# Moving the split weight pieces inside their ring rows, and x and the masks with them, in a four-layer decoder trunk

## The chip, the cores and the metric

The kernel runs on one core of one Trainium2 chip. The metric is the device time of one execution in microseconds (us). Engines are named as the profile names them: PE is TensorE (matmuls), PEld its weight loads, DVE is VectorE, ACT is ScalarE, POOL is GpSimd, SP is SyncE, which here issues most DMA transfers. L560 is line 560 of the kernel before.

## The reference, cut to what matters

The trunk has four layers on a (1, 256, 1024) float32 input. Each layer is an FFN, a token mixer and another FFN; every one of these twelve sub-layers is wrapped in two RMSNorms:

```
x = x + 0.5 * rmsnorm(swiglu(rmsnorm(x, g0), wg, wu, wd), g1)      # FFN, D_FF = 2816
x = x + rmsnorm(mixer(rmsnorm(x, g2)), g3)                         # conv, attention, mLSTM, conv
x = x + 0.5 * rmsnorm(swiglu(rmsnorm(x, g4), wg, wu, wd), g5)
```

The conv mixer projects to 3 x 1024, gates, convolves with three taps and projects out. The attention mixer projects to three groups of q, k and v (16 heads of 64), attends in three dilated causal windows, mixes them by their log-sum-exp and projects out. The mLSTM mixer projects to q, k, v, an output gate and eight gate columns, runs a stabilised matrix memory and projects out. All weights are float32.

## The kernel before

**Split products.** Every float32 weight and activation is split into a high part (rounded to the type fp32r) and a low part (the rest). One product is three fp32r matmuls: high by high, high by low, low by high. A matmul has a stationary operand (loaded 128x128, PEld) and a moving operand (256 or 512 columns), and the weight load of the next matmul runs while the present one streams its moving operand.

**Pieces and rings.** All weights come as one stream of 352 pieces of 128 x 2048 float32 (`PIECE` = 2048 words a partition). SP loads piece p into `raw[p % 3]`. ACT writes its high part to `w_high[p % 6]` (L1215), DVE writes `raw - w_high` to `w_low[p % 6]` (L1660), PE multiplies, and the semaphores `piece_high`, `piece_split` and `piece_used` keep the order. `RING` is 6, and before the change a ring row is exactly one piece, 8192 bytes a partition.

**Two ways round.** A piece is multiplied in one of two ways. *Features-first*: the weights are stationary and x (`xT_both`, which holds the transposed high and low x, 256 tokens) is the moving operand; so run the blocks of the FFNs (`block`, L560 to L562) and most pieces of the mixers (`features_half`, L574 to L576). *Tokens-first*: 128 tokens of x are stationary and the piece's columns move. In the mixers these are 256 columns (`tokens_first`, L574 to L576, and `arriving`, L587 to L593); in the FFNs the first four pieces (`early_block`, L560 to L562 and `arriving`) with 512 columns. Tokens-first pieces are: the first three of each mixer (`first_three`), the v pieces of attention (three of nine in each quarter, the first three of quarter 0 among them) and pieces 7 to 11 of mLSTM. The down and output projections move weights of 512 columns past `oT_hi` and `oT_lo`; they are not touched.

**Where things lie.** SBUF tensors are allocated in order: `raw`, `w_high`, `w_low`, `oT_hi`, `oT_lo`, `x`, `xn`, `gain`, each a multiple of 8192 bytes a partition, then six small ones that take 32 bytes each, then `xT_both`. So `xT_both` begins 192 bytes (48 words) past a multiple of 8192 from the start of each ring row, and `oT_hi` at a multiple. In mLSTM alone, `X_SHIFT` puts x 32 words (128 bytes) further into `xT_both`.

**The turn of x.** At a sub-layer's start the second 128 tokens of x are still being normed. PE runs two and a half tokens-first pieces on the first tile, waits for `xn` (L1708 on DVE, the end of a chain over ACT, DVE and POOL), makes eight transposes (L609), and goes on. `products_at_entry` (L568 to L570) is a form of the product that cuts the first of its three matmuls into two of 128 columns; it is used at a few places behind transposes or a change of piece, in `first_three` for mLSTM alone.

**Masks and gains.** `att_mask`, `ml_mask` and `tri` are loaded by SP behind the twelfth piece. ACT loads two gain vectors in each joint (`load_gains`, L1337 and L1339).

Of the kernel before, what the change touches and what calls it, by code (L numbers as in the profile page):

```python
# [24 lines left out]
F32R = mybir.dt.float32r  # L25
# [3 lines left out]
P = 128  # L29
# [46 lines left out]
X_SHIFT = {"ffn": 0, "conv": 0, "att": 0, "ml": 32}  # L76
# [68 lines left out]

def build(nc, x_in, gains, first_gain, stream, gate_w, gate_b, conv_k, ident_in, rope_in, att_mask_in, ml_mask_in,
          tri_in, out):
    with ExitStack() as ctx:
# [10 lines left out]
        w_high = sb("w_high", [P, RING, PIECE], F32R)  # L159
        w_low = sb("w_low", [P, RING, PIECE], F32R)  # L160
# [65 lines left out]
        ml_mask = sb("ml_mask", [P, 2 * P])  # L226
        tri = sb("tri", [P, P])
# [23 lines left out]
        loaded = sem("loaded")  # L251
        raw_landed = [sem(f"raw_landed{n}") for n in range(RAW)]
# [87 lines left out]
        CONSTS = 16 * 7  # L340
# [177 lines left out]
        def _(sp):  # L518
# [13 lines left out]
            sp.dma_start(ml_mask[:, :], ml_mask_in).then_inc(loaded, 16)  # L532
            sp.dma_start(tri[:, :], tri_in).then_inc(loaded, 16)
# [19 lines left out]
        def _(pe):  # L553
# [24 lines left out]
            def arriving(acc, joint, t, half, p, width, first_col):  # L578


                tok, slot = slice(t * P, (t + 1) * P), p % RING
# [4 lines left out]
                for k, cols in rows:  # L586
                    nc.tensor.matmul(acc, xT_high()[:, k, tok], w_high[:, slot, cols], start=k == 0, stop=False)  # L587
                x_ready(joint, t, half)
                for k, cols in rows:
                    nc.tensor.matmul(acc, xT_low()[:, k, tok], w_high[:, slot, cols], start=False, stop=False)  # L590
                weights_ready(p)
                for k, cols in rows:
                    last = nc.tensor.matmul(acc, xT_high()[:, k, tok], w_low[:, slot, cols], start=False, stop=k == KD - 1)  # L593
# [27 lines left out]
            def ffn(sub):  # L621
# [13 lines left out]
                def early_block(i, first_x=False, meanwhile=None):  # L635
# [3 lines left out]
                    for half in range(2):  # L639
                        p = w0 + early_piece(c) + half  # L640
                        slot = p % RING
# [4 lines left out]
                        for k in () if first_x else range(4 * half, 4 * half + 4):  # L646
# [3 lines left out]
                                            w_high[:, slot, cols], w_low[:, slot, cols], k == 0, k == KD - 1)  # L650
# [7 lines left out]
                def block(i, p, turn=0):  # L658
# [3 lines left out]
                    for e in range(2):  # L662
                        for k in range(KD):
                            cols = slice(k * 256 + e * P, k * 256 + (e + 1) * P)
                            last = products(ps[:, gu_bank(i), e * SEQ:(e + 1) * SEQ], w_high[:, p % RING, cols],
                                            w_low[:, p % RING, cols], xT_high()[:, k, :], xT_low()[:, k, :],
                                            k == 0, k == KD - 1)
                    last.then_inc(piece_used, 1)

                def first_blocks():  # L670

                    x0, slot = slice(0, P), 0
# [3 lines left out]
                    for k, cols in rows[0:2]:  # L676
                        nc.tensor.matmul(ps[:, GU_BANK, :], xT_high()[:, k, x0], w_high[:, slot, cols], start=k == 0, stop=False)
                    transpose_x(0, 1)
                    x_ready(0, 0, 0)
                    for k, cols in rows[0:2]:  # L680
                        nc.tensor.matmul(ps[:, GU_BANK, :], xT_low()[:, k, x0], w_high[:, slot, cols], start=False, stop=False)
                    pe.wait_ge(piece_high, 1)
                    for k, cols in rows[2:4]:
                        nc.tensor.matmul(ps[:, GU_BANK, :], xT_high()[:, k, x0], w_high[:, slot, cols], start=False, stop=False)
                        nc.tensor.matmul(ps[:, GU_BANK, :], xT_low()[:, k, x0], w_high[:, slot, cols], start=False, stop=False)
                    pe.wait_ge(first_split, 1)
                    for k, cols in rows:
                        if k == 2:
                            weights_ready(0)
                        nc.tensor.matmul(ps[:, GU_BANK, :], xT_high()[:, k, x0], w_low[:, slot, cols], start=False, stop=False)  # L690
# [14 lines left out]
                def seven(c, some, turn=0):  # L705
# [11 lines left out]
                    for n in some:  # L717
# [7 lines left out]
                        else:  # L725
                            rh, rl = w_high[:, p % RING, cols], w_low[:, p % RING, cols]
# [1642 lines left out]
```

## Time and profile before

| what | value |
|---|---|
| median of 3 runs | 1981.74 us (1981.50 to 1982.76) |
| the profiled execution | 1981.68 us, span 1979.1 us |
| PE busy | 1971.2 us |
| DVE busy | 1619.8 us |
| ACT busy | 1103.9 us |

The profiled execution took 1981.68 us as timed; its span, from the first to the last instruction, is 1979.1 us, so 2.58 us lie around the span. [...] A line of the source view gives a line's instructions in a stretch: count, smallest, median and largest duration in ns, and the start of the first and of the last. In mixers three matmuls lie between two starts of L574 (the three parts of a product).

### The profile page before, as it was taken

The page shows a single profiled execution, that of the slowest core. Times are in us where ns is not written, and L with a number is a line of the kernel's source. Part 1 is how long each engine was busy: PE and PEld are TensorE (multiplying, and loading weights), DVE is VectorE, ACT ScalarE, POOL GpSimd, SP SyncE. Part 2 cuts the span into 40 slices and gives each one's busy share as a digit, 9 for nine tenths or more (in the row PEclk, how much of TensorE's full clock was granted, in tenths as well). Part 3 has the DMA queues.
Part 4 walks back from the last instruction along what each step waited for, and adds up shares of the span by engine and source line. Part 5 has one row for each costly group of instructions (what it writes and reads, how often), then busy time and mean ns, then how long its engine had stood idle before and what let it go on. Part 6 is the DMA issues. An engine that isn't in the chain of part 4 may idle for free.

```text
span 1979.1 us, 36338 instructions
## 1 busy us (share of the span) xinstructions
PE 1971.2 (100%) x14806; PEld 1839.8 (93%) x14806; DVE 1619.8 (82%) x1865; ACT 1103.9 (56%) x1208; POOL 26.5 (1%) x52
## 2 busy tenths in 40 slices
PE   9999999999999999999999999999999999999998
PEld 8999989998999999988998999998999899998998
DVE  8988678888888777769898888657888888777886
ACT  6555445555555665666555556645555555545553
POOL 0000000000000000000000000000000000000000
PEclk9999999999999999999999999999999999999999
DMA  7655645564555644435555556534556456654552
GB/s 265 246 212 202 228 170 192 193 243 159 210 212 196 213 172 153 168 129 191 213 200 208 189 196 248 215 130 149 213 192 233 171 207 227 215 183 157 213 191 107
DMA packets 56289, 386.35 MB, mean 195 GB/s; under 512 B 6752, under 2 KB 7136, under 8 KB 11232
## 3 DMA queue, kind: packets, MB, share of 16 engines
q1 hardware_dynamic: 52416, 372.07, 51.6%
q10 hardware_dynamic: 3744, 12.39, 2.0%
q8 instruction: 102, 1.67, 0.3%
q14 instruction: 27, 0.22, 0.0%
HBM read 383.39 MB, written 1.05 MB: 194 GB/s over the span
## 4 chain that ended last, share of the span: by engine, by line
PE 97%; DVE 1%; DMA 1%; issue 0%; ACT 0%; POOL 0%; DVEq 0%; POOLq 0%; SPq 0%
PE ps L560 21%; PE ps L561 21%; PE ps L562 21%; PE ps L574 6%; PE ps L575 6%; PE ps L576 6%; PE ps L590 2%; PE ps L587 2%; PE ps L593 2%; PE ps L739 1%; PE ps L736 1%; PE ps L735 1%; PE ps L609 1%; PE ps L965 0%; PE ps L700 0%
## 5 line engine op out<-in xcount | busy, mean ns | idle before, releaser
L1660 DVE TENSOR_TENSOR w_low<-raw,w_high 128x2048 fp32r<-128x2048 f32 x272 | 616.3, 2286 | 87.4 <-ACT w_high L1215 87.4
L560 PE MATMUL ps<-xT_both,w_high 128*128 128x256 f32 x2304 | 638.4, 277 | 0.0
L561 PE MATMUL ps<-xT_both,w_high 128*128 128x256 f32 x2304 | 637.1, 277 | 0.0
L562 PE MATMUL ps<-xT_both,w_low 128*128 128x256 f32 x2304 | 636.6, 276 | 0.0
L1215 ACT ACTIVATE w_high<-raw 128x2048 fp32r<-128x2048 f32 x279 | 530.6, 1912 | 39.9 <-DMA raw<-stream 27.4
L561 PEld LDWEIGHTS ps<-xT_both,w_high 128*128 128x128 f32 x2304 | 433.3, 188 | 0.0
L562 PEld LDWEIGHTS ps<-xT_both,w_low 128*128 128x128 f32 x2304 | 432.7, 188 | 0.0
L560 PEld LDWEIGHTS ps<-xT_both,w_high 128*128 128x128 f32 x2304 | 432.5, 188 | 0.1
L1261 ACT ACTIVATE region<-ps 128x256 f32<-128x256 f32 x176 | 67.4, 383 | 439.2 <-PE ps L562 431.7
L574 PE MATMUL ps<-xT_both,w_high 128*128 128x256 f32 x729 | 204.9, 281 | 0.0
L575 PE MATMUL ps<-xT_both,w_low 128*128 128x256 f32 x729 | 202.6, 278 | 0.0
L576 PE MATMUL ps<-xT_both,w_high 128*128 128x256 f32 x729 | 202.5, 278 | 0.0
L1733 DVE TENSOR_TENSOR region<-region,ps 128x256 f32<-128x256 f32 x176 | 73.8, 419 | 131.9 <-ACT region L1261 129.6
L560 PE MATMUL ps<-w_high,oT_hi 128*128 128x512 f32 x456 | 179.1, 393 | 0.0
L561 PE MATMUL ps<-w_low,oT_hi 128*128 128x512 f32 x456 | 177.9, 390 | 0.0
L562 PE MATMUL ps<-w_high,oT_lo 128*128 128x512 f32 x456 | 177.9, 390 | 0.0
L1292 ACT ACTIVATE w_high<-xn 128x2048 fp32r<-128x2048 f32 x72 | 138.2, 1919 | 27.3 <-DVE xn L1773 25.8
L1786 DVE TENSOR_TENSOR w_low<-xn,w_high 128x2048 fp32r<-128x2048 f32 x64 | 146.4, 2287 | 4.8 <-ACT w_high L1292 4.8
L574 PEld LDWEIGHTS ps<-xT_both,w_high 128*128 128x128 f32 x729 | 137.3, 188 | 0.7
L575 PEld LDWEIGHTS ps<-xT_both,w_low 128*128 128x128 f32 x729 | 137.2, 188 | 0.0
L576 PEld LDWEIGHTS ps<-xT_both,w_high 128*128 128x128 f32 x729 | 137.0, 188 | 0.0
L1779 DVE TENSOR_TENSOR corner<-raw,corner 128x1536 fp32r<-128x1536 f32 x72 | 126.1, 1752 | 0.0
(239 smaller groups left out, 3140.3 us busy)
## 6 DMA issues: line engine op xcount, KB each, us to landing
raw<-stream SPq DMA_DIRECT2D x351, 1024.0 KB, 4.8
gain<-gains ACTq DMA_DIRECT2D x23, 512.0 KB, 4.9
x<-x_in SPq DMA_DIRECT2D x2, 512.0 KB, 4.5
raw<-stream SPq DMA_DIRECT2D x2, 512.0 KB, 6.2
region<-rope_in SPq DMA_DIRECT2D x1, 512.0 KB, 5.1
out<-x SPq DMA_DIRECT2D x1, 512.0 KB, 2.6
att_mask<-att_mask_in SPq DMA_DIRECT2D x1, 320.0 KB, 5.5
out<-x SPq DMA_DIRECT2D x1, 256.0 KB, 2.1
```

The lines of the kernel that those rows point to most:

```text
L560: nc.tensor.matmul(acc, lh, rh, start=start, stop=False, skip_group_check=goes_on)
L561: nc.tensor.matmul(acc, lh, rl, start=False, stop=False, skip_group_check=goes_on)
L562: return nc.tensor.matmul(acc, ll, rh, start=False, stop=stop, skip_group_check=goes_on)
L574: nc.tensor.matmul(acc, lh, rh, start=start, stop=False)
L575: nc.tensor.matmul(acc, ll, rh, start=False, stop=False)
L576: return nc.tensor.matmul(acc, lh, rl, start=False, stop=stop)
L1215: nc.scalar.activation(w_high[:, p % RING, :], raw[:, p % RAW, :], ACT.Copy).then_inc(piece_high, 1)
L1292: nc.scalar.activation(w_high[:, p % RING, :], sums, ACT.Copy).then_inc(piece_high, 1)
L1660: nc.vector.tensor_tensor(w_low[:, p % RING, :], raw[:, p % RAW, :], w_high[:, p % RING, :], ALU.subtract).then_inc(piece_split, 1)
L1733: nc.vector.tensor_tensor(h_of(i) if i >= EARLY else h[:, i % 2, :], silu[:, i % 2, :], ps[:, gu_bank(i), SEQ:2 * SEQ], ALU.mult).then_inc ...
L1779: nc.vector.tensor_tensor(corner[:, c % 2, 1, :], raw[:, p % RAW, HALF:4 * HALF], corner[:, c % 2, 0, :], ALU.subtract).then_inc(piece_spl ...
L1786: nc.vector.tensor_tensor(w_low[:, p % RING, :], sums, w_high[:, p % RING, :], ALU.subtract).then_inc(sums_split, 1)
```

## The change

- A ring row gets 64 words (256 bytes) more: `ROW = PIECE + 64`, for `w_high` and `w_low`. A piece begins in its row at `w_shift(p)`: 41 words (164 bytes) in for the first four pieces of an FFN, 32 words (128 bytes) for tokens-first pieces of mixers, 0 for all others. ACT, DVE and PE use that place through `high_of(p)` and `low_of(p)`.
- x lies at the start of `xT_both` in every sub-layer; mLSTM's 32 words are gone (the tensor keeps its size).
- `products_at_entry` is used at the turn of x in conv and attention too (`halves_at=4 if turns`), and at the start of mLSTM's feature pieces 4, 5 and 6 (`i > 3`).
- `ml_mask` and `tri` have no tensors of their own: they are views of `att_mask`, loaded by ACT in the joint behind attention, after the last masking (`masked`), ahead of the gains there. SP has two constant loads fewer, and DVE and PE wait for `masks_landed` in mLSTM.

```diff
-X_SHIFT = {"ffn": 0, "conv": 0, "att": 0, "ml": 32}
+X_PAD = 32
+ROW = PIECE + 64
+W_SHIFT = {"early": 41, "tokens": 32}
...
+def w_shift(p):
+
+    sub = max(n for n in range(SUBLAYERS) if BASE[n] <= p)
+    q, kind = p - BASE[sub], KINDS[sub]
+    if kind == "ffn":
+        return W_SHIFT["early"] if q < EARLY else 0
+    if kind == "att":
+        tokens = q < QP * QUARTERS and not 1 <= ATT_ORDER[q // QP][q % QP] <= QK
+    else:
+        tokens = q < 3 or kind == "ml" and 7 <= q < 12
+    return W_SHIFT["tokens"] if tokens else 0
...
-        w_high = sb("w_high", [P, RING, PIECE], F32R)
-        w_low = sb("w_low", [P, RING, PIECE], F32R)
+        w_high = sb("w_high", [P, RING, ROW], F32R)
+        w_low = sb("w_low", [P, RING, ROW], F32R)
+
+        def place(p):
+
+            first = w_shift(p)
+            return slice(first, first + PIECE)
+
+        def high_of(p):
+            return w_high[:, p % RING, place(p)]
+
+        def low_of(p):
+            return w_low[:, p % RING, place(p)]
...
-        xT_both = sb("xT_both", [P, 2 * KD * SEQ + max(X_SHIFT.values())], F32R)
+        xT_both = sb("xT_both", [P, 2 * KD * SEQ + X_PAD], F32R)
...
-            at = X_SHIFT[KINDS[sub_now[0]]] + which * KD * SEQ
-            return xT_both[:, at:at + KD * SEQ].rearrange("p (k c) -> p k c", k=KD)
+            return xT_both[:, which * KD * SEQ:(which + 1) * KD * SEQ].rearrange("p (k c) -> p k c", k=KD)
...
-        ml_mask = sb("ml_mask", [P, 2 * P])
-        tri = sb("tri", [P, P])
+        ml_mask = att_mask[:, 0:2 * P]
+        tri = att_mask[:, 2 * P:3 * P]
...
-            sp.dma_start(ml_mask[:, :], ml_mask_in).then_inc(loaded, 16)
-            sp.dma_start(tri[:, :], tri_in).then_inc(loaded, 16)
...
-                        done = tokens_first(p % RING, acc, t, meanwhile=(lambda: transpose_x(sub, 1)) if turns else None,
-                                            halves_at=4 if turns and KINDS[sub] == "ml" else None)
+                        done = tokens_first(p, acc, t, meanwhile=(lambda: transpose_x(sub, 1)) if turns else None,
+                                            halves_at=4 if turns else None)
...
-                    features_first((w0 + i) % RING, bank).then_inc(piece_used, 1)
+                    features_first(w0 + i, bank, i > 3).then_inc(piece_used, 1)
...
                 pe.wait_ge(ml_copied, 6)
+                pe.wait_ge(masks_landed, 32)
...
-                nc.scalar.activation(w_high[:, p % RING, :], raw[:, p % RAW, :], ACT.Copy).then_inc(piece_high, 1)
+                nc.scalar.activation(high_of(p)[:, :], raw[:, p % RAW, :], ACT.Copy).then_inc(piece_high, 1)
...
+                if joint and KINDS[joint - 1] == "att":
+                    act.wait_ge(masked, 4 * QUARTERS)
+                    act.dma_start(ml_mask, ml_mask_in).then_inc(masks_landed, 16)
+                    act.dma_start(tri, tri_in).then_inc(masks_landed, 16)
                 act.dma_start(gain[:, 0, :], gains[2 * joint + 1].partition_broadcast(P)).then_inc(gain_landed, 16)
...
                 dve.wait_ge(loaded, CONSTS)
+                dve.wait_ge(masks_landed, 32)
```

Every other line of the diff puts `high_of(p)` or `low_of(p)` where `w_high[:, p % RING, ...]` or `w_low[:, p % RING, ...]` stood.

## Rows read from the trace of the kernel before

**Rows 1.** The page: busy time in us of each engine, share of the span, instructions.
```profile
PE 1971.2 (100%) x14806; PEld 1839.8 (93%) x14806; DVE 1619.8 (82%) x1865; ACT 1103.9 (56%) x1208; POOL 26.5 (1%) x52
```

**Rows 2.** The page, chain that ended last: shares of the span by engine.
```profile
PE 97%; DVE 1%; DMA 1%; issue 0%; ACT 0%; POOL 0%; DVEq 0%; POOLq 0%; SPq 0%
```

**Rows 3.** Waits of PE: for whom, us in total, times, longest us.
```profile
PE ps L609 <- DVE xn L1708: 0.2, 1, 0.2
```

**Rows 4.** Source view of L574, first conv: a tokens-first, then a features-first stretch.
```profile
L574 PE MATMUL ps<-w_high,xT_both x16: 279/279/279, 199.8 to 205.1; 128*128 128x256 f32 x16
...
L574 PE MATMUL ps<-xT_both,w_high x92: 276/276/276, 212.0 to 243.0; 128*128 128x256 f32 x92
```

**Rows 5.** Source view of L574, mLSTM: tokens-first, two features-first stretches, tokens-first.
```profile
L574 PE MATMUL ps<-w_high,xT_both x16: 276/276/276, 1258.5 to 1263.6; 128*128 128x256 f32 x16
...
L574 PE MATMUL ps<-xT_both,w_high x16: 276/276/276, 1265.8 to 1270.9; 128*128 128x256 f32 x16
...
L574 PE MATMUL ps<-xT_both,w_high x15: 278/280/280, 1272.0 to 1277.0; 128*128 128x256 f32 x15
...
L574 PE MATMUL ps<-w_high,xT_both x15: 281/281/281, 1303.3 to 1308.2; 128*128 128x256 f32 x15
```

**Rows 6.** Source view of L574: conv behind transposes, attention's features, attention's tokens-first.
```profile
L574 PE MATMUL ps<-xT_both,w_high x31: 281/281/281, 245.0 to 255.6; 128*128 128x256 f32 x31
...
L574 PE MATMUL ps<-xT_both,w_high x74: 276/276/276, 657.9 to 682.7; 128*128 128x256 f32 x74
...
L574 PE MATMUL ps<-w_high,xT_both x16: 279/279/387, 741.7 to 747.1; 128*128 128x256 f32 x16
```

**Rows 7.** Timeline of PE (start us, us): early blocks, then down projection, of sub-layer 2.
```profile
297.14 0.39 PE L560 MATMUL ps<-w_high,xT_both 128*128 128x512 f32 x1
...
301.72 0.39 PE L562 MATMUL ps<-w_high,xT_both 128*128 128x512 f32 x1
...
443.16 0.39 PE L560 MATMUL ps<-w_high,oT_hi 128*128 128x512 f32 x1
...
447.70 0.39 PE L562 MATMUL ps<-w_high,oT_lo 128*128 128x512 f32 x1
```

**Rows 8.** Timelines of DVE and PE at the turn of x: conv, mLSTM, an FFN.
```profile
193.24 1.29 DVE L1708 SCALAR_TENSOR_TENSOR xn<-x,rstd_x,gain 128x1024 f32<-128x1024 f32 x1 [0.66 <-POOL rstd_x L2256]
...
194.62 1.05 PE L609 MATMUL ps<-ident,xn 128*128 128x128 f32 x8
...
1252.03 1.28 DVE L1708 SCALAR_TENSOR_TENSOR xn<-x,rstd_x,gain 128x1024 f32<-128x1024 f32 x1 [0.66 <-POOL rstd_x L2256]
...
1253.38 1.09 PE L609 MATMUL ps<-ident,xn 128*128 128x128 f32 x8
...
284.64 1.28 DVE L1708 SCALAR_TENSOR_TENSOR xn<-x,rstd_x,gain 128x1024 f32<-128x1024 f32 x1 [0.66 <-POOL rstd_x L2256]
...
287.54 1.03 PE L609 MATMUL ps<-ident,xn 128*128 128x128 f32 x8
```

**Rows 9.** Timeline of PE behind those transposes: conv without the cut, mLSTM with it.
```profile
195.44 0.36 PE L574 MATMUL ps<-w_high,xT_both 128*128 128x256 f32 x1
...
195.87 0.28 PE L574 MATMUL ps<-w_high,xT_both 128*128 128x256 f32 x1
...
1254.22 0.42 PE L568 MATMUL ps<-w_high,xT_both 128*128 128x128 f32 x2
...
1254.77 0.28 PE L574 MATMUL ps<-w_high,xT_both 128*128 128x256 f32 x1
```

**Rows 10.** Timelines of ACT and PE in the joint behind attention.
```profile
902.46 0.97 ACTq L1339 DMA_DIRECT2D gain<-gains  x1
...
904.16 0.39 ACT L1261 ACTIVATE region<-ps 128x256 f32<-128x256 f32 x1 [1.42 <-PE ps L562]
...
909.67 0.38 PE L700 MATMUL ps<-ident,region 128*128 128x128 f32 x2
```

**Rows 11.** Source view of the conv's shifted taps on DVE, L2025.
```profile
L2025 DVE SCALAR_TENSOR_TENSOR region<-region,conv_kT x32: 476/481/485, 218.0 to 1772.9; 128x256 f32<-128x256 f32 x32
```

More of the change, by code:

```diff
@@ L338, in build @@
         stored = sem("stored")
-        CONSTS = 16 * 7
+        CONSTS = 16 * 5
         used[0] = 0
@@ L586, in arriving @@
                 for k, cols in rows:
-                    nc.tensor.matmul(acc, xT_high()[:, k, tok], w_high[:, slot, cols], start=k == 0, stop=False)
+                    nc.tensor.matmul(acc, xT_high()[:, k, tok], high_of(p)[:, cols], start=k == 0, stop=False)
                 x_ready(joint, t, half)
                 for k, cols in rows:
-                    nc.tensor.matmul(acc, xT_low()[:, k, tok], w_high[:, slot, cols], start=False, stop=False)
+                    nc.tensor.matmul(acc, xT_low()[:, k, tok], high_of(p)[:, cols], start=False, stop=False)
                 weights_ready(p)
                 for k, cols in rows:
-                    last = nc.tensor.matmul(acc, xT_high()[:, k, tok], w_low[:, slot, cols], start=False, stop=k == KD - 1)
+                    last = nc.tensor.matmul(acc, xT_high()[:, k, tok], low_of(p)[:, cols], start=False, stop=k == KD - 1)
                 return last
@@ L664, in block @@
                             cols = slice(k * 256 + e * P, k * 256 + (e + 1) * P)
-                            last = products(ps[:, gu_bank(i), e * SEQ:(e + 1) * SEQ], w_high[:, p % RING, cols],
-                                            w_low[:, p % RING, cols], xT_high()[:, k, :], xT_low()[:, k, :],
+                            last = products(ps[:, gu_bank(i), e * SEQ:(e + 1) * SEQ], high_of(p)[:, cols],
+                                            low_of(p)[:, cols], xT_high()[:, k, :], xT_low()[:, k, :],
                                             k == 0, k == KD - 1)
@@ L670, in first_blocks @@
                 def first_blocks():
-                    x0, slot = slice(0, P), 0
+                    x0, p = slice(0, P), 0
                     rows = [(k, slice(k * 512, (k + 1) * 512)) for k in range(4)]
@@ L676, in first_blocks @@
                     for k, cols in rows[0:2]:
-                        nc.tensor.matmul(ps[:, GU_BANK, :], xT_high()[:, k, x0], w_high[:, slot, cols], start=k == 0, stop=False)
+                        nc.tensor.matmul(ps[:, GU_BANK, :], xT_high()[:, k, x0], high_of(p)[:, cols], start=k == 0, stop=False)
                     transpose_x(0, 1)
@@ L680, in first_blocks @@
                     for k, cols in rows[0:2]:
[L681 removed]
+                        nc.tensor.matmul(ps[:, GU_BANK, :], xT_low()[:, k, x0], high_of(p)[:, cols], start=False, stop=False)
                     pe.wait_ge(piece_high, 1)
                     for k, cols in rows[2:4]:
[L684 to L685 removed]
+                        nc.tensor.matmul(ps[:, GU_BANK, :], xT_high()[:, k, x0], high_of(p)[:, cols], start=False, stop=False)
+                        nc.tensor.matmul(ps[:, GU_BANK, :], xT_low()[:, k, x0], high_of(p)[:, cols], start=False, stop=False)
                     pe.wait_ge(first_split, 1)
@@ L689, in first_blocks @@
                             weights_ready(0)
-                        nc.tensor.matmul(ps[:, GU_BANK, :], xT_high()[:, k, x0], w_low[:, slot, cols], start=False, stop=False)
+                        nc.tensor.matmul(ps[:, GU_BANK, :], xT_high()[:, k, x0], low_of(p)[:, cols], start=False, stop=False)
                     arriving(ps[:, GU_BANK + 1, :], 0, 1, 0, 0, 512, 0).then_inc(piece_used, 1)
@@ L793, in chunk @@
                             transpose_next(sub, (1,))
-                            return nc.tensor.matmul(acc, oT_lo[:, at, tok], w_high[:, p % RING, cols], start=False, stop=True,
+                            return nc.tensor.matmul(acc, oT_lo[:, at, tok], high_of(p)[:, cols], start=False, stop=True,
                                                     skip_group_check=True)
                         last = products(ps[:, Y_BANK + 2 * t + half, :], oT_hi[:, at, tok], oT_lo[:, at, tok],
-                                        w_high[:, p % RING, cols], w_low[:, p % RING, cols], False, ends, goes_on=True)
+                                        high_of(p)[:, cols], low_of(p)[:, cols], False, ends, goes_on=True)
                     return last
@@ L820, in project_out @@
                     for q in range(first if t == 0 else 0, OUT_PIECES):
-                        slot = (p0 + q) % RING
-                        weights_ready(p0 + q)
+                        p = p0 + q
+                        weights_ready(p)
                         if t == 0 and q % 2 == 0:
@@ L835, in project_out, with features_half @@
                             last.then_inc(y_ready, 1)
-            def features_half(slot, acc, j, behind_transposes=False):
+            def features_half(p, acc, j, behind_transposes=False):
                 for k in range(KD):
@@ L856, in tokens_first @@
                     multiply = products_at_entry if k == halves_at else products_in_turn
-                    last = multiply(acc, xT_high()[:, k, tok], xT_low()[:, k, tok], w_high[:, slot, cols],
-                                    w_low[:, slot, cols], k == 0, k == KD - 1)
+                    last = multiply(acc, xT_high()[:, k, tok], xT_low()[:, k, tok], high_of(p)[:, cols],
+                                    low_of(p)[:, cols], k == 0, k == KD - 1)
                     if meanwhile and k == 3:
```

54 lines of the change are left out of this document (27 added, 27 removed).

## The prediction, made before the change was run

> **What bounds the kernel now.** The page comes first: PE is busy for 1971.2 of 1979.1 us [rows 1], and the chain that ended last lies on PE for 97% [rows 2]. The waits of PE say whether another engine holds it up: behind its start it waits once, 0.2 us, for `xn` at the turn of x in mLSTM [rows 3]. So a matmul that starts 1 ns sooner is worth up to 1 ns, except where a wait stands ready to take it. PE's durations overlap and tell little, so the third view is the source view of single lines, for the distance between starts. There the same 256-column matmul runs at two paces:
>
> - First conv, tokens-first: 5.3 us over 15 x 3 matmuls, 117.8 ns each; features-first: 31.0 over 273, 113.6 ns [rows 4]. The recorded duration marks the pace too: 279 to 281 ns in the slow one, 276 in the fast.
> - mLSTM, where x lies 32 words further, has it the other way round: tokens-first 5.1/45 = 113.3 ns; features-first fast at first (113.3), then slow (5.0/42 = 119) [rows 5].
>
> The reader should see one quantity behind both: how far, modulo 64 words, the moving operand lies from the stationary operand that is being loaded for the next matmul. x begins 48 words past a ring row (modulo 64), so features-first (x moves) has 48 and tokens-first (weights move) has -48 = 16. With x 32 words further it is 80 = 16 for features-first and -80 = 48 for tokens-first. So 48 tends to the fast pace and 16 to the slow. It is a tendency: a stretch keeps the pace it came in with. Features at 16 stayed fast for a whole piece behind a fast one [rows 5]; features at 48 ran slow at 10.6/90 = 117.8 ns behind transposes and at 24.8/219 = 113.2 ns behind a cut product; attention's tokens-first matmuls at 16 are slow behind its scores (the 387 ns is the first one) [rows 6], and one of mLSTM's token stretches at 48 is slow too [rows 5].
>
> **The change part by part.** After it, x at 0 and weights at 32 give tokens-first 16 + 32 = 48 in all mixers, features-first 48 everywhere, and the FFNs' early pieces 16 + 41 = 57. I take the difference of the paces as 4.5 ns (117.8 - 113.3).
>
> *FFN early pieces.* 96 matmuls of 512 columns in each of 8 FFNs. At 16 they take (301.72 - 297.14)/20 = 229.0 ns; the down projection, the same shape at distance 0, (447.70 - 443.16)/20 = 227.0 [rows 7]. No row has 57. It lies between 48 and 64, which is 0 again, 7 words from the 0 that is fast, so I take 227: 768 x 2.0 ns = 1.5 us. Bounds: nothing, and about 2 us if the few slow ones behind each interruption go too. The cover: the transposes there start 1.6 us behind the end of L1708 (284.64 + 1.28, then 287.54) [rows 8], so no wait takes it back.
>
> *First three pieces of conv (twice) and attention, before the turn.* Some 58 matmuls could give 0.26 us, but the norm chain does not get shorter. In conv L1708 ends at 194.53 and the transposes start at 194.62, 0.09 us behind; in mLSTM, which already runs fast here, they start 0.07 us behind and PE has waited [rows 8]. So 0.02 us is to be had, three times: 0.06 us. The stall of mLSTM appears in the others.
>
> *The same pieces behind the turn.* 81 matmuls at 4.5 ns: 0.36 us. The cut product comes in: from its start to the next product 0.55 us in mLSTM against 0.43 uncut in conv [rows 9], so it costs 0.12. Net 0.24, three times: 0.7 us. Bounds 0 and 1.1.
>
> *Attention's later v pieces.* Nine pieces, 432 matmuls. Read the same way, six stretches with 240 matmuls are slow now, of which one row stands here [rows 6]; the others came in fast and stay so. 240 x 4.5 ns = 1.1 us if all turn. They come behind scores, and at 48 a stretch can still come in slow [rows 5, 6]; I take half, 0.5 us, and 0 and 1.1 as bounds.
>
> *mLSTM.* Three of four feature pieces, 138 matmuls, are slow at 16 [rows 5]; at 48 with a cut at their start they may turn: 0.6 us, against 3 x 0.12 = 0.36 us for the cuts. A cut has been followed by a fast stretch where no transposes stood before it and by a slow one behind eight transposes [rows 6]; piece 4 has two small ones before it, piece 5 six small f32 products, piece 6 eight. I take two of three: 0.42 - 0.36 = 0.06, and 0.15 for the token piece behind them. Together 0.2 us, bounds -0.36 and 0.7.
>
> *At nothing.* The DVE and ACT writes at odd words: the conv taps read `cu` 0, 1 and 2 words in and take 476 to 485 ns all the same [rows 11]; if a row of weights were slower by some ns, DVE (82% busy) hides it. Masks: two more issues on ACT in the joint behind attention, up to 0.97 us each as the second gain took there, so 1.94 us. ACT is free from 903.43 (902.46 + 0.97) to 904.16, where PE releases the silu [rows 10]; the silu comes up to 1.2 us late. What is made of it is next needed by the transposes at 909.67 [rows 10], 5.1 us behind the end of the silu, so PE does not see it; without that cover the 1.2 us would count. `masked` was reached before the joint, and the masks land hundreds of us ahead of mLSTM, so their two waits are free. SP has two issues fewer, early, where PE does not wait.
>
> Sum: 1.5 + 0.06 + 0.7 + 0.5 + 0.2 = 3.0 us. From the profiled execution's 1981.68 us that is 1978.7; the median, 1981.74, differs by 0.06, so I predict 1978.7 us, 0.15% faster. A measurement of this kernel can tell about 0.2% (4.0 us) from no change, so this counts as the same.
>
> **The rivals.** *More of the slow pace goes.* All 240 and all 138 turn, the token stretches of mLSTM with them (95 x 4.5 = 0.4), and FFN takes 2: 2.0 + 0.8 + 1.1 + 0.6 + 0.4 - 0.36 = 4.5 us, 1977.2. And since a stretch hands its pace on, attention's features that are slow now could follow (some 440 at 4.5 ns, 2 us): 1975.2. For it speaks that fast stretches last for 219 matmuls and more [rows 6], against it that most of attention's stretches begin behind an interruption, which 48 does not cure.
>
> *Place does not matter.* The paces would come from what ran before and not from where things lie. Then only the six cuts are left, 0.7 us: 1982.4. Rows 4 and 5 speak against it, since the swap of the two ways in mLSTM would be an accident; the hysteresis in rows 5 and 6 speaks for it. [...]
>
> *Rows of odd slots go slow.* I took the relation as repeating every 64 words; rows before show only distances whose step of 128 is harmless. With 256 bytes more a row, features-first in every second slot gets 48 - 64 = -16. If the relation repeats only after 128 words, that is a distance that no row shows. It concerns half of the features-first matmuls (48 a piece: 144 pieces in the FFNs' blocks, 18 in the convs, 24 in attention, 4 in mLSTM, 9120 in all): 4560 x 4.5 ns = 20.5 us, less the gain, 1999.2. It decides the sign once some 670 of them (3.0 us / 4.5 ns) are slow. Against it: under 128 words, 0 and 48 are fast and only 80 slow, and -16 lies beside 0.
>
> **How the numbers follow.** The forecast, 1.5 to 4 us saved: 0.44. More of the slow pace goes: 0.37, nearly all past 4 us. Place does not matter, or its gain is under 1.5 us: 0.11. Odd slots slow: 0.08. So faster by over 0.2%: 0.37; within 0.2%: 0.54; slower: 0.09, the last hundredth for a wait I overlook. The range, 1975.0 to 1982.4, takes in the three cases on the fast side and their bounds and leaves out the odd slots. The forecast's own range is 1977.7 to 1980.2.
>
> **What would show it.** Right: the source view has 276 ns and 113 to 114 ns pace for tokens-first in both convs; the early pieces run at 227; PE waits 0.2 us for L1708 in conv and attention too; L568, two records a cut, has six more at the turns of x and six more in mLSTM. Wrong: L574 stays at 279 behind the turn (the cut did not help); the early pieces stay at 229 (57 is not like 0); FFN blocks at 281 in every second slot (the third rival); L700 at about 909.67 late against its block (the masks' issues).

## The result and the profile after

The changed kernel takes 1986.12 us (median; 1985.73 to 1987.01) against 1981.74 for the kernel before, which ran on the same chips: ratio 1.0022, 95% interval 1.0015 to 1.0030. It is slower by 4.4 us, where 3 us less were forecast, and outside the range.

The page of the changed kernel, busy time and chain, beside [rows 1, 2]:

```profile
PE 1976.9 (100%) x14812; PEld 1841.4 (93%) x14812; DVE 1620.2 (82%) x1865; ACT 1104.6 (56%) x1208; POOL 26.6 (1%) x52
...
PE 99%; issue 0%; DVE 0%; DMA 0%; ACT 0%; POOL 0%; DVEq 0%; POOLq 0%
```

The span grew by 5.3 us (1984.4 against 1979.1) and PE's busy time by 5.7, with six matmul records more, the six cuts. The busy times of the others grew by 1.6 us or less. PE's waits (for whom, us in total, times, longest us):

```profile
PE ps L580 <- DVE ones L1681: 1.1, 1, 1.1
PE ps L633 <- DVE xn L1733: 0.3, 1, 0.3
PE ps L700 <- ACT xT_both L1266: 0.3, 1, 0.3
```

They come to 1.7 us, all in the kernel's first 11 us, where the same view of before lists 2.5. So nobody holds PE up more than before; the matmuls themselves start further apart. In the changed kernel lines 560 to 562 are 584 to 586, 574 to 576 are 598 to 600, 587 to 593 are 611 to 617, and 609 is 633. The timeline of PE over the early pieces of sub-layer 2 (start us, recorded us): the first of them, two that stand for those of [rows 7], and the first features-first matmul behind them.

```profile
279.43 1.11 PE L611 MATMUL ps<-w_high,xT_both 128*128 128x512 f32 x4
...
298.52 0.40 PE L584 MATMUL ps<-w_high,xT_both 128*128 128x512 f32 x1
...
303.25 0.40 PE L586 MATMUL ps<-w_high,xT_both 128*128 128x512 f32 x1
...
303.62 0.37 PE L584 MATMUL ps<-xT_both,w_high 128*128 128x256 f32 x1
```

Between 298.52 and 303.25 lie 20 distances of 236.5 ns (the records of 0.40 us overlap), where [rows 7] had 229.0. From the first early matmul to the first features-first one it is 303.62 - 279.43 = 24.19 us. Call this length S; it holds the 96 early matmuls and the few transposes between them, the same in every kernel. Its two ends before the change:

```profile
278.62 1.07 PE L587 MATMUL ps<-w_high,xT_both 128*128 128x512 f32 x4
...
302.09 0.37 PE L560 MATMUL ps<-xT_both,w_high 128*128 128x256 f32 x1
```

Before the change S is 302.09 - 278.62 = 23.47 us, and 23.44 to 23.49 in the six other FFNs behind the first. After it, it is 0.69 to 0.73 us longer in each of the seven, 5.0 us in all, or 0.72 us / 96 = 7.5 ns a matmul. In the first FFN, whose S varies with the kernel's start (below), it is 0.75 us longer. With it the sum is 5.75 us, the span's whole growth and 0.4 us more.

The mixers' turn and their stretches: the first conv's timeline of DVE and PE at the turn (beside [rows 8, 9]), then the source views of L598 in the first conv (tokens, features behind them), attention (two tokens-first stretches) and mLSTM (tokens ahead of the turn and behind it).

```profile
194.09 1.28 DVE L1736 SCALAR_TENSOR_TENSOR xn<-x,rstd_x,gain 128x1024 f32<-128x1024 f32 x1 [0.66 <-POOL rstd_x L2285]
...
195.43 1.09 PE L633 MATMUL ps<-ident,xn 128*128 128x128 f32 x8
196.28 0.42 PE L592 MATMUL ps<-w_high,xT_both 128*128 128x128 f32 x2
...
196.82 0.28 PE L598 MATMUL ps<-w_high,xT_both 128*128 128x256 f32 x1
```
```profile
L598 PE MATMUL ps<-w_high,xT_both x18: 276/276/276, 197.2 to 205.7; 128*128 128x256 f32 x18
...
L598 PE MATMUL ps<-xT_both,w_high x17: 276/281/286, 206.7 to 212.8; 128*128 128x256 f32 x17
...
L598 PE MATMUL ps<-w_high,xT_both x16: 281/281/283, 685.7 to 691.0; 128*128 128x256 f32 x16
...
L598 PE MATMUL ps<-w_high,xT_both x15: 276/276/277, 734.0 to 738.7; 128*128 128x256 f32 x15
...
L598 PE MATMUL ps<-w_high,xT_both x12: 281/281/281, 1252.7 to 1256.6; 128*128 128x256 f32 x12
...
L598 PE MATMUL ps<-w_high,xT_both x18: 276/276/276, 1258.6 to 1267.1; 128*128 128x256 f32 x18
```

Tokens-first in the first conv runs fast now, as forecast (276 for the 279 of [rows 4]), but the features behind it came in slow. In attention one stretch turned from slow to fast and others from fast to slow; mLSTM's first tokens became slow. Paces changed places.

The FFNs' features-first blocks, source view of L584 in the last FFN, all slots of the ring:

```profile
L584 PE MATMUL ps<-xT_both,w_high x128: 276/276/286, 1836.6 to 1899.1; 128*128 128x256 f32 x128
```

And the engines' granted clock, in a window of those blocks in sub-layer 2 (stretch; its length; busy us and count of PE, PEld, DVE, ACT, POOL; granted clock; DMA share; GB/s):

```profile
310.00:330.00 20.00, 20.00 (x140) 18.48 (x139) 19.22 (x19) 12.94 (x10) 0.00 (x0) 1.00 0.50 180
```

It is 1.00, as in the same window of before (1.00), so the loss isn't one of the clock.

### The profile page after: what moved, and what is told of

It reads as the page before. It is cut to its first block, busy times and chain, and to the rows that moved or that the text cites. A ratio compares the mean times of both kernels' runs of the same rounds, so it can differ in the third digit from the quotient of the medians.

```text
span 1984.4 us, 36350 instructions
## 1 busy us (share of the span) xinstructions
PE 1976.9 (100%) x14812; PEld 1841.4 (93%) x14812; DVE 1620.2 (82%) x1865; ACT 1104.6 (56%) x1208; POOL 26.6 (1%) x52
## 4 chain that ended last, share of the span: by engine, by line
PE 99%; issue 0%; DVE 0%; DMA 0%; ACT 0%; POOL 0%; DVEq 0%; POOLq 0%
PE ps L584 22%; PE ps L586 22%; PE ps L585 22%; PE ps L598 6%; PE ps L600 6%; PE ps L599 6%; PE ps L614 2%; PE ps L611 2%; PE ps L617 2%; PE ps L762 2%; PE ps L758 1%; PE ps L759 1%; PE ps L633 1%; PE ps L988 0%; PE ps L723 0%
## 5 line engine op out<-in xcount | busy, mean ns | idle before, releaser
L1688 DVE TENSOR_TENSOR w_low<-raw,w_high 128x2048 fp32r<-128x2048 f32 x272 | 616.3, 2286 | 89.8 <-ACT w_high L1239 89.8
L584 PE MATMUL ps<-xT_both,w_high 128*128 128x256 f32 x2304 | 638.1, 277 | 0.0
L1239 ACT ACTIVATE w_high<-raw 128x2048 fp32r<-128x2048 f32 x279 | 530.7, 1912 | 42.1 <-DMA raw<-stream 29.4
L584 PEld LDWEIGHTS ps<-xT_both,w_high 128*128 128x128 f32 x2304 | 432.5, 188 | 0.0
L598 PE MATMUL ps<-xT_both,w_high 128*128 128x256 f32 x726 | 203.7, 281 | 0.0
L584 PE MATMUL ps<-w_high,oT_hi 128*128 128x512 f32 x456 | 179.1, 393 | 0.0
L598 PEld LDWEIGHTS ps<-xT_both,w_high 128*128 128x128 f32 x726 | 136.6, 188 | 0.7
```

Of the source, the lines that this page charges most:

```text
L584: nc.tensor.matmul(acc, lh, rh, start=start, stop=False, skip_group_check=goes_on)
L598: nc.tensor.matmul(acc, lh, rh, start=start, stop=False)
L1239: nc.scalar.activation(high_of(p)[:, :], raw[:, p % RAW, :], ACT.Copy).then_inc(piece_high, 1)
L1688: nc.vector.tensor_tensor(low_of(p)[:, :], raw[:, p % RAW, :], high_of(p)[:, :], ALU.subtract).then_inc(piece_split, 1)
```

## The experiments

The theories of each run stand in its expectation. Times are medians with the ratio to the kernel before on the same chip; where only one time is given, it is a single one and the lengths S carry the verdict. Beside these runs the kernel before took 1981.35 to 1981.64 us. Gains and losses of an FFN are its S less the S of the same FFN before. The first FFN's S is left out of verdicts, since the kernel's start lies in it: in the four kernels below with its early pieces at 0 it came out between 0.36 us shorter and 0.33 us longer than before.

**Early pieces back at 0** (rest of the change kept), and **rows and masks alone** (mixers, x and cuts as before too).

```diff
-W_SHIFT = {"early": 41, "tokens": 32}
+W_SHIFT = {"early": 0, "tokens": 32}
```
```diff
-W_SHIFT = {"early": 41, "tokens": 32}
+W_SHIFT = {"early": 0, "tokens": 0}
+X_SHIFT = {"ffn": 0, "conv": 0, "att": 0, "ml": 32}
...
+                                            halves_at=4 if turns and KINDS[sub] == "ml" else None)
...
+                    features_first(w0 + i, bank).then_inc(piece_used, 1)
```

> The changed kernel with the FFNs' early pieces back at the start of their rows, all else as changed. Theory: the whole loss is theirs, 8 times 0.7 us; the kernel takes 5.7 us less than the changed one, 1980.4 us, 0.05 to 0.1% under the kernel before. Rival: the longer rows or the masks cost something too; then it stays at 1982 us or over.

> The longer rows and the late masks alone: every piece at the start of its row, x in mLSTM 32 words further, cut products as before. Theory: 256 bytes more a row and the late masks cost nothing: 1981.7 us, and features-first in odd slots at 113 to 114 ns. Rival (odd slots, a relation that repeats only after 128 words): features-first at 118 ns in every second slot, up to 20 us more.

Early at 0: 1981.28 us, ratio 1.0000 (0.9991 to 1.0009). Rows and masks alone: 1981.65, ratio 1.0001 (0.9992 to 1.0010). The first lies 0.9 us above its theory's 1980.4 and under its rival's 1982. So the loss goes with the 41, and of what was forecast for the mixers nothing shows in the times, which tell 0.09% either way.

**The 41 alone**, with rows and masks, on mixers, x and cuts as before (the second diff above, but for one number).

```diff
-W_SHIFT = {"early": 41, "tokens": 32}
+W_SHIFT = {"early": 41, "tokens": 0}
```

> The kernel with longer rows and late masks, and the FFNs' early pieces at 41 words; mixers' pieces, mLSTM's x and the cuts as before. Theory 'the place 41 alone costs it': the early pieces' matmuls start 239 ns apart where before has 232, 0.7 us in each of 8 FFNs, so 5.7 us more than before: 1987.3 us, ratio 1.0029, if anything above the changed kernel's 1986.1, since the mixers' edits gave back 0.4 us by the traces. Rival 'it takes the cuts and the mixers' move as well' (the pace in which a mixer ends is handed on into the next FFN): under half of it, below 1984 us.

1986.65 us, ratio 1.0026 (1.0016 to 1.0036). S is 0.69 to 0.73 us longer in the seven FFNs, to 0.01 us the same as in the changed kernel. The rival falls: the early pieces need nothing else to be slow.

**Other places for the early pieces**, another one in each FFN of a kernel; the three lists are three kernels, in the order of the expectations below.

```diff
+EARLY_SHIFT = {0: 40, 2: 0, 3: 16, 5: 32, 6: 40, 8: 44, 9: 48, 11: 56}
+EARLY_SHIFT = {0: 42, 2: 1, 3: 2, 5: 41, 6: 42, 8: 43, 9: 33, 11: 57}
+EARLY_SHIFT = {0: 43, 2: 3, 3: 47, 5: 51, 6: 59, 8: 48, 9: 63, 11: 64}
...
-        return W_SHIFT["early"] if q < EARLY else 0
+        return EARLY_SHIFT[sub] if q < EARLY else 0
```

> Each FFN's early pieces get a place of their own, all multiples of four words: 40, 0, 16, 32, 40, 44, 48, 56 words for the eight FFNs in order (sub-layers 0, 2, 3, 5, 6, 8, 9, 11), so distances of 56, 16, 32, 48, 56, 60, 0 and 8 modulo 64. Theory: a moving operand that does not begin on a multiple of four words (16 bytes) is read more slowly; then all eight FFNs run their early pieces at 226 to 230 ns a matmul and take about 177.0 us each, and 40, one word from 41, is as fast as 0. Rival: 57 is a bad distance; then 40 and 44 (56 and 60) run at 234 to 240 ns and take 177.7 us, the others not.

> The same with places that are not multiples of four, but for two of them multiples of two: 42, 1, 2, 41, 42, 43, 33, 57 words for the eight FFNs in order. Theory (16-byte grid): all eight run at 234 to 240 ns a matmul whatever the distance, 0.6 to 0.8 us a FFN more than the multiples. Were the grid 8 bytes, the three at 42, 2 and 42 would run at 229. Rival (distance): 1, 2 and 33 (distances 17, 18, 49) run as 16 and 48 do, at 227 to 230; only 41 to 43 are slow.

> The changed kernel with the early pieces of its eight FFNs at 43, 3, 47, 51, 59, 48, 63 and 64 words, in this order. Theory 'the rest by 4 decides': a rest of 3 costs nothing, as 43 did (0.0 us in its FFN), so 43, 3, 47, 51, 59 and 63 all come out at 232 ns and 0.0 us, 48 at 231 and -0.1, 64 as 0 does: together 1981.5 us. Rival 'single places are good' (0, 43 and 48 by chance, the others cost 0.35 to 0.9 us as 16, 32, 40, 44, 56 and the even and odd ones did): 3, 47, 51, 59 and 63 come out at 235 to 241 ns, together 1983 to 1986 us. A place whose cost follows its distance to the nearest of the good ones (47 by 48, 63 by 64: small; 3 and 59: larger) would be what the prediction thought of.

The kernels took 1982.26, 1985.87 and 1981.26 us, single times. Timelines of PE, first early matmul and first features-first one: at 32 words (sub-layer 5 of the first), then at 1 and at 43 words (sub-layers 2 and 8 of the second).

```profile
892.89 1.10 PE L612 MATMUL ps<-w_high,xT_both 128*128 128x512 f32 x4
...
916.75 0.37 PE L585 MATMUL ps<-xT_both,w_high 128*128 128x256 f32 x1
```
```profile
278.70 1.12 PE L612 MATMUL ps<-w_high,xT_both 128*128 128x512 f32 x4
...
303.10 0.37 PE L585 MATMUL ps<-xT_both,w_high 128*128 128x256 f32 x1
...
1354.53 1.08 PE L612 MATMUL ps<-w_high,xT_both 128*128 128x512 f32 x4
...
1377.99 0.36 PE L585 MATMUL ps<-xT_both,w_high 128*128 128x256 f32 x1
```

S is 23.86, 24.40 and 23.46 us, where before had 23.44, 23.47 and 23.44 in these FFNs. All places read in this way, loss of an FFN in us (1 us / 96 = 10.4 ns a matmul):

| rest of the place by 4 | places and loss |
|---|---|
| 0 | 0: -0.03 to 0.03; 48: -0.12 and -0.10; 64: 0.00; 16: 0.32; 44 and 56: 0.34; 40: 0.36; 32: 0.41 |
| 3 | 63: -0.04; 43: 0.02; 51: 0.06; 59: 0.08; 47: 0.11; 3: 0.17 |
| 2 | 2: 0.42; 42: 0.47 |
| 1 | 41: 0.69 to 0.76; 57: 0.76; 1 and 33: 0.92 |

One reading at 0 is not in the table: 0.28, in the FFN behind attention of the kernel with the mixers apart (below), where a wait of PE lies in S. No simple rule holds. A grid of four words would make all rests but 0 dear and 40 as cheap as 0; a rest of 3 is nearly free, and 40 costs 0.36. A distance to a good place would make 1 and 47 cheap next to 0 and 48, and 1 is the dearest of all. What the table does show is that 41 is one of the worst places, and that 32, where x and weights lie at the relation that the prediction took for fast, costs 0.41 us here.

**The early pieces at 48 alone**, the best place of the table; mixers, x and cuts as before.

```diff
-W_SHIFT = {"early": 41, "tokens": 32}
+W_SHIFT = {"early": 48, "tokens": 0}
```

> As the kernel with the early pieces alone moved, but to 48 words where that had 41. If a place's price is a property of the place, the 0.12 us that one FFN gained at 48 comes eight times: 1.0 us less than before, 1980.7 us, ratio 0.9995, with 231 ns between starts in every FFN. Rival, the price is that of the place in one FFN only (what ran before it sets it): mixed signs, within 1 us of before, or slower.

1980.44 us, ratio 0.9995 (0.9986 to 1.0004): by the times not to be told from before. S is 0.12 us shorter in five of the seven FFNs, 0.10 and 0.02 in the others. So in six of the seven the price goes with the place, whatever places the other FFNs have. In the FFN behind attention nearly nothing is gained (0.02 here, 0.01 in the last kernel below), so what ran before it can have a part in the price; how is not shown.

**x moved as well**, per FFN, to tell the place of the weights from their relation to x.

```diff
-X_PAD = 32
+X_PAD = 64
+X_SHIFT = {2: 41, 3: 41, 5: 1, 6: 1, 8: 32, 9: 32, 11: 48}
+EARLY_SHIFT = {0: 0, 2: 41, 3: 0, 5: 0, 6: 1, 8: 41, 9: 0, 11: 48}
...
-            return xT_both[:, which * KD * SEQ:(which + 1) * KD * SEQ].rearrange("p (k c) -> p k c", k=KD)
+            at = X_SHIFT.get(sub_now[0], 0) + which * KD * SEQ
+            return xT_both[:, at:at + KD * SEQ].rearrange("p (k c) -> p k c", k=KD)
```

> The changed kernel with places of x and of the early pieces chosen per FFN (x / early pieces, in words): 0/0, 41/41, 41/0, 1/0, 1/1, 32/41, 32/0, 48/48. Theory 'the relation of the weights to x counts': the early matmuls of 41/41, 1/1 and 48/48 come out like 0/0 at 232 ns, 32/41 like a place of 9 with a rest of 1 (239 to 241), 32/0 like a place of 32 away (236), 41/0 and 1/0 away from 232. Theory 'the place of the moving weights by itself counts': 41/41, 1/1 and 32/41 stay at 239 to 242 whatever x does, 41/0, 1/0 and 32/0 come out at 232, 48/48 at 231. The features-first matmuls, in which x moves and the weights lie at 0, tell the same from the other side: by the second theory they become slower in the FFNs with x at 41 and 1 (114 ns before), by the first too. Total 1982 to 1990 us.

2023.1 us once, where 1982 to 1990 was expected. Timelines of PE, first early and first features-first matmul, with x / early pieces at 41/41, 41/0, 32/0 and 48/48; between the first pair's rows and the second's, two features-first matmuls of a block with x at 41.

```profile
278.87 1.11 PE L614 MATMUL ps<-w_high,xT_both 128*128 128x512 f32 x4
...
303.10 0.36 PE L587 MATMUL ps<-xT_both,w_high 128*128 128x256 f32 x1
...
315.86 0.28 PE L587 MATMUL ps<-xT_both,w_high 128*128 128x256 f32 x1
...
318.40 0.28 PE L587 MATMUL ps<-xT_both,w_high 128*128 128x256 f32 x1
...
463.07 1.08 PE L614 MATMUL ps<-w_high,xT_both 128*128 128x512 f32 x4
...
486.57 0.36 PE L587 MATMUL ps<-xT_both,w_high 128*128 128x256 f32 x1
...
1561.77 1.10 PE L614 MATMUL ps<-w_high,xT_both 128*128 128x512 f32 x4
...
1585.63 0.37 PE L587 MATMUL ps<-xT_both,w_high 128*128 128x256 f32 x1
...
1834.03 1.09 PE L614 MATMUL ps<-w_high,xT_both 128*128 128x512 f32 x4
...
1857.51 0.36 PE L587 MATMUL ps<-xT_both,w_high 128*128 128x256 f32 x1
```

S against before: 41/41 costs 0.76 us, 1/1 0.73 and 32/41 0.76, as the places with a rest of 1 do with x at 0, though x and weights stand to each other as at 0/0 in the first two. 41/0 costs 0.04. So at places with a rest of 1 it is in the main the place of the moving weights that counts (1 costs 0.92 with x at 0, so x may have a part). Among the multiples of 16 tried here it is the relation: 48/48 costs 0.00 like 0/0 (0/48 gains 0.12), and 32/0 costs 0.37, beside 0.41 for 0/32, which is the same relation modulo 64 words. Each theory is right for a part of the places. With the weights at 0, x at 1 costs 0.41, as the relation would have it, and x at 41 costs 0.04, as the place would; that stays open.

The other side is dearer, and it is why the time was missed. With x at 41 the features-first matmuls, in which x moves, stand (318.40 - 315.86)/21 = 121.0 ns apart in a block, against 113.6 in [rows 4]. Summed over the starts in an FFN, its 864 such matmuls became 5.9 to 6.1 us slower with x at 41, 6.8 to 7.0 with x at 1, 2.9 to 3.1 at 32 and 4.4 at 48. The tensors behind x moved by 32 words too here, and the products with `corner` cost 0.3 us more in each FFN.

**The mixers, piece by piece.** By the traces of the changed kernel and those with its mixers, a stretch of tokens-first that begins directly behind features-first, with nothing between, always had the other pace than the features had (first starts 117.8 ns apart behind 113.3 at four sites of the changed kernel); with the mixers as before it always had the same (113.3 behind 113.3 at three sites of the kernel before, 117.8 behind 117.8 at the fourth). One kernel with different places in each mixer, and one in which a single switch was moved.

The first has, by quarter of attention, the places of the list (with the cut at attention's turn), the first conv at 0 with the cut, mLSTM's and the second conv's at 32 without cuts:

```diff
+W_SHIFT = {"early": 0, "tokens": 32}
+V_SHIFT = [32, 0, 16, 48]
...
+        return V_SHIFT[q // QP] if tokens else 0
```

The second is the kernel with early pieces at 48 and the mixers as before, but for pieces 7 and 8 of attention's second quarter:

```diff
-        tokens = q < QP * QUARTERS and not 1 <= ATT_ORDER[q // QP][q % QP] <= QK
+        tokens = QP + 7 <= q < 2 * QP
+        return 32 if tokens else 0
```

> Early pieces at 0. Tokens-first pieces: first conv at 0 words but with the cut at the turn; attention's first quarter at 32, its second at 0, its third at 16, its fourth at 48; mLSTM's and the second conv's at 32, without any of the cuts. Theory 'a stretch takes the pace of the one before; a switch of way keeps it where x and weights lie as before the change (0) and turns it over where the weights lie 32 words further': the second quarter's tokens come in fast behind fast features at about 685.7 us (slow in the changed kernel) and behind slow features stay slow at 733; the first conv's features behind its tokens keep their pace; the second conv's turn theirs over. Rival 'place chooses the pace': the second quarter is slow wherever it stands, the fourth, 64 words from x, fast. Either way within 1.5 us of 1981.3 us.

> The kernel with the early pieces at 48 and the mixers as before, and of attention's second quarter the last two v pieces 32 words further, which come behind slow features at about 731 us. Theory 'a move by 32 turns the pace over at the switch from features to tokens': these 72 matmuls come in fast, 113.3 ns where they had 117.8, 0.3 us less; what the features behind them do it doesn't say (their first 24 were fast in five kernels behind slow tokens). So 1979.8 to 1980.7 us, ratio 0.9993, not to be told from the 0.9995 without it; the verdict lies in the pace behind 731 us alone. Rival: they stay slow, and the pace has another cause.

The first took 1982.04 us once. Its second quarter, at 0, kept both paces: 276 ns recorded behind features of 276 at 683.5 us, 280 behind features of 281 at 731.2. mLSTM's, at 32, turned slow into fast at 1291.3. The third and fourth quarters, at 16 and 48, came in slow behind fast features (118.8 and 120.0 ns behind 113.3). The rival expected slow in the second quarter and fast in the fourth; of these it got one of the second's two stretches. The theory's part on features behind tokens missed twice: in the first conv, which was to keep its pace, slow became fast (117.7 to 113.5 ns), and in the second conv, which was to turn it over, slow stayed slow (117.8 ns).

The other took 1980.01 us, ratio 0.9993 (0.9984 to 1.0002). Source views of the first 18 products behind the switch near 731 us: with the early pieces at 48 alone, then with this one switch moved.

```profile
L600 PE MATMUL ps<-w_high,xT_both x18: 280/280/282, 731.0 to 737.0; 128*128 128x256 f32 x18
```
```profile
L601 PE MATMUL ps<-w_high,xT_both x18: 276/276/286, 730.9 to 736.7; 128*128 128x256 f32 x18
```

The features ahead are slow in both; the tokens are slow where the weights keep their place, (737.0 - 731.0)/51 = 118 ns, and fast where they move by 32, 5.8/51 = 114. So the move turns the pace over, as foreseen. Over all traces, read from the distances of the starts, there are 26 switches of this kind with the weights unmoved: 16 fast behind fast, 10 slow behind slow, none else. With the weights moved by 32 there are 32: 25 from fast to slow, 7 from slow to fast, none else. They are the same five sites of the kernel again and again, four in attention and one in mLSTM; the kernel with the one switch moved is the test that was foretold. The switch from tokens to features has no such rule here: with the weights unmoved, features behind slow tokens (117.8 ns) came in slow or fast: 113.3 ns in the first conv of the kernel before, 117.8 in its second.

## Why the prediction was wrong

**The step that failed is the early pieces' place.** The prediction put them at 57 of a cycle of 64 words, said that "it lies between 48 and 64, which is 0 again", and took 227 ns for 229, 1.5 us gained, with nothing as the lower end. Measured is 236.5 ns, 7.5 ns a matmul lost: 5.0 us in the seven FFNs behind the first by the trace, and over all eight 5.0 us in the times when 41 is put in and 4.5 when it is taken out (4.4 us above before become 0.1 under it). Three things were wrong in it:

- One neighbour was read wrongly. That 48 is fast came from 256-column matmuls in mixers; for the early pieces the relation 48 is the weights at 32, and that costs 0.41 us an FFN. Of the relations tried only 64, the weights at 48, is clearly better than before (0.12 and 0.10 us less in the table).
- Single words were not thought of. The rows showed places at multiples of 16 words only; 41 has a rest of 1 by 4, and all four places with that rest that were tried cost 0.69 to 0.92 us wherever x lay. A value between two known points was no estimate for a place of another kind.
- The lower bound "nothing" excluded a loss without a reason. The same text asked what distances that no row shows would cost, for odd slots; asked of 57, with the mixers' 4.5 ns for 768 matmuls, the answer would have been a loss of 3.5 us and, with nothing from the mixers, 1985.2: still short, since 7.5 ns stood in no row, but on the right side.

**The mixers' terms** (0.06 + 0.7 + 0.5 + 0.2 = 1.5 us) did not come: with the early pieces at 0 the rest of the change measured 1.0000 of before, where (1981.7 - 1.5)/1981.7 = 0.9992 was expected, just inside the interval of 0.9991 to 1.0009. The trace of the changed kernel tells more: from its first matmul to the next sub-layer's, the first conv took 0.03 us less than before, attention 0.24 more, mLSTM 0.01 less and the second conv 0.10 less, so together 0.1 us was lost where 1.5 was to be gained. (With the mixers as before, three kernels summed to 0.1 less to 0.4 more.) The tendency read in [rows 4, 5] was taken for a property of the place; it was a pace that came in from before. The same places give both paces: the tokens-first matmuls ahead of the first conv's turn, with x at 0 and weights at 32, in the changed kernel and in the one with the early pieces back at 0:

```profile
L598 PE MATMUL ps<-w_high,xT_both x12: 276/276/276, 191.2 to 194.9; 128*128 128x256 f32 x12
```
```profile
L598 PE MATMUL ps<-w_high,xT_both x12: 281/281/281, 191.3 to 195.2; 128*128 128x256 f32 x12
```

Ahead of mLSTM's turn it is the other way round, slow (281 ns) in the first and fast (276) in the second, though the prediction's distance there is 48 in both, and was 48 before. The remark that "a stretch keeps the pace it came in with" stood in the prediction, and should have had the weight that the place got: at the switch from features to tokens the move by 32 swapped the two paces whichever of them came in, and in attention three of four such switches came in fast before.

**The cut** cost what was said: 196.82 - 196.28 = 0.54 us to the next product, for 0.43 without it [rows 9]. Behind it the first conv's tokens ran fast (113.3 ns), attention's and the second conv's slow (117.8), so one of three of that term came. Of mLSTM's three new cuts two were followed by fast features, as taken, but the tokens behind the last came in slow, and the mixer as a whole, from its first matmul to the next sub-layer's, took 105.14 us for 105.15; source view of L598 there:

```profile
L598 PE MATMUL ps<-xT_both,w_high x15: 281/281/281, 1275.7 to 1280.6; 128*128 128x256 f32 x15
...
L598 PE MATMUL ps<-xT_both,w_high x15: 276/276/276, 1282.1 to 1286.9; 128*128 128x256 f32 x15
...
L598 PE MATMUL ps<-xT_both,w_high x15: 276/276/279, 1288.5 to 1293.3; 128*128 128x256 f32 x15
...
L598 PE MATMUL ps<-w_high,xT_both x16: 281/281/282, 1293.6 to 1298.9; 128*128 128x256 f32 x16
```

The stall named for the turn came in the first conv: the transposes start 0.06 us behind the end of `xn` (194.09 + 1.28 = 195.37, then 195.43), and 0.30 us behind the start of the last product, 0.12 before. It came in attention and the second conv too (0.30 us each), and went from mLSTM, whose first tokens are slow now (0.12 for 0.30). The view of waits above doesn't list it. The wait of 0.2 us in [rows 3], which the prediction put at mLSTM's turn, lies elsewhere in the trace of before, at the entry of an FFN (sub-layer 9); no term rests on it, only the sign that such a wait would show in conv and attention.

```profile
195.13 0.28 PE L600 MATMUL ps<-w_low,xT_both 128*128 128x256 f32 x1
```
```profile
1527.34 0.66 PE L609 MATMUL ps<-ident,xn 128*128 128x128 f32 x4 [0.15 <-DVE xn L1708]
```

**What was costed at nothing** was nothing in the changed kernel. The means of the high and the low parts of the pieces are 1912 and 2286 ns as before, so odd words, in 32 of the pieces, cost ACT and DVE a few ns each at most. The masks' issues and the silu behind them on ACT:

```profile
904.67 0.33 ACTq L1363 DMA_DIRECT2D att_mask<-ml_mask_in  x1
...
905.04 0.81 ACTq L1364 DMA_DIRECT2D att_mask<-tri_in  x1
...
906.86 0.39 ACT L1285 ACTIVATE region<-ps 128x256 f32<-128x256 f32 x1 [1.55 <-PE ps L586]
```

They took 1.14 us, not 1.94, and the silu still waited for PE, not for them; rows and masks alone measured 1.0001. The cover is thin, though. In the kernel with the mixers apart the issue behind the masks' and the first gain's took 1.33 us, the silu waited for the issues, and two blocks later PE's loads for the transposes waited for DVE, whose work from that silu on pauses for 0.3 us only: the transposes start 0.41 us behind the last product (916.16, then 916.57) for 0.24 before. It is the only one of eleven kernels with late masks where this shows.

```profile
904.91 1.33 ACTq L1369 DMA_DIRECT2D gain<-gains  x1
906.28 0.39 ACT L1287 ACTIVATE region<-ps 128x256 f32<-128x256 f32 x1 [2.58 <-issue]
...
916.57 0.20 PEld L725 LDWEIGHTS ps<-ident,region 128*128 128x128 f32 x2 [0.45 <-DVE region L1763]
```

**The rivals.** *More of the slow pace goes* is out (attention's slow features come to 408 matmuls in the trace of before, not 440, so its 2 us was 1.8). *Rows of odd slots go slow* is out: the blocks of the last FFN show a median of 276 ns over 128 products and none above 286, and longer rows with the late masks measured 1.0001. *Place does not matter* came nearest in the mixers and is wrong for the FFNs: early pieces at 1 cost 0.92 us in an FFN, against 0.00 at 0. The case that happened, the early pieces slower at 41 than at 0, was not among the rivals; the sign named for a failure there was that they stay at 229 ns.

What stays open is the mechanism. The runs show which places are dear, that a rest of 1 is dear wherever x lies (0.69 to 0.92 us), and that the multiples of 16 tried go by the relation to x (0.00 for 48/48, 0.37 and 0.41 for 32/0 and 0/32); they don't show why a rest of 3 is nearly free and 16 and 32 are not (-0.04 to 0.17 against 0.32 and 0.41 us), nor why x at 1 costs the early pieces 0.41 us and x at 41 0.04.

## What to carry to other kernels

Where PE sets the end, the place of a moving operand in its row is worth up to 10 ns a matmul here (0.92 us / 96), and it can't be read from neighbours (0.92 us at 1, 0.00 at 0): try a few places, one in each repeat of a sub-layer, in one kernel, and read each from the distance of starts. Before a difference of pace is put down to a place, look at what stands ahead of the stretch: here a stretch came in with a pace (113.3 or 117.8 ns), and a change of place at a switch turned it over, for good or ill. A place that no row shows has a lower bound on the loss side too.

## What the hardware showed

- 512 columns moving from places 0, 48, 43 and 41 of a row take 96 matmuls in 23.47, 23.35, 23.46 and 24.19 us (S, turn included); 256 columns of x moving from 41 words further stand 121.0 ns apart instead of 113.6.
- At the switch from features-first to tokens-first in mixers, weights at the same place keep the pace (113.3 or 117.8 ns) and weights 32 words further swap it, at all 58 such switches of these traces (five sites of the kernel).
- The best kernel run, early pieces at 48 and one stretch turned, took 1980.01 us, 0.9993 of before (0.9984 to 1.0002): not to be told from it.
